# Conditioning pieces 4 and 5 moved ahead in a hybrid diffusion trunk kernel

## The reference, cut to what matters

```
def _adaln(cond, w, b):
    m = jax.nn.silu(cond) @ w + b
    return [t[:, None, :] for t in jnp.split(m, 6, axis=-1)]   # shift, scale, gate for mixer and feed-forward
...
hp = _modulate(_rms(xp, norm_mix[l]), m_ctx[0], m_ctx[1])      # x * (1 + scale) + shift
... mixer: layer 0 attention and short conv, layer 1 Conformer convolution
xp = xp + m_ctx[2] * op
hp = _modulate(_rms(xp, norm_ffn[l]), m_ctx[3], m_ctx[4])
... layer 0: dense SwiGLU (2816 wide); layer 1: top-2 of 8 experts (3584 wide each)
xp = xp + m_ctx[5] * fp

def _conformer_conv(h, p):
    z = h @ p["w_pw1"] + p["b_pw1"];  a, g = jnp.split(z, 2, axis=-1);  u = a * jax.nn.sigmoid(g)
    u = depthwise_conv(u, 31 taps) + p["b_dw"];  u = jax.nn.silu(_layernorm(u, p["ln_g"], p["ln_b"]))
    return u @ p["w_pw2"] + p["b_pw2"]
```

## Time and profile before

| what | value |
| --- | --- |
| three runs | 1481.68, 1483.83, 1489.67 us; median 1483.83 |
| the profiled execution's own time | 1483.04 us |
| its span, first to last instruction | 1481.3 us |
| granted TensorE clock, mean | 0.996 |
| TensorE busy | 1439.8 us (97%) |
| VectorE, ScalarE, GpSimd busy | 1148.8, 935.3, 59.2 us |
| bytes moved | 478.93 MB, mean 323 GB/s |

### The profile page before, as it was taken

The page is one execution under the profiler, slowest core; times in us unless marked ns, Lnnn a source line. Parts: engine busy times, 40 slices in busy tenths (PEclk is TensorE's granted clock), DMA queues, the critical chain, the costliest instruction groups (busy, mean ns, idle before and its releaser), DMA issues.

```text
span 1481.3 us, 20338 instructions
## 1 busy us (share of the span) xinstructions
PE 1439.8 (97%) x8408; PEld 1211.8 (82%) x8408; DVE 1148.8 (78%) x1075; ACT 935.3 (63%) x888; POOL 59.2 (4%) x61
## 2 busy tenths in 40 slices
PE   6999999999989999999999999999999999999997
PEld 4778899998967778888888888888888888888885
DVE  3565744445876699889978989888888987988997
ACT  2454643333415687777777777787777777777773
POOL 0210000001221100000000000000000000001010
PEclk9999999999999999999999999999999999999999
DMA  9867766656795499999989999989999999999993
GB/s 371 300 239 276 266 226 228 228 181 224 245 300 181 156 360 373 373 387 375 378 349 374 373 379 380 377 337 391 376 369 394 373 377 348 376 373 381 400 402 135
DMA packets 103570, 478.93 MB, mean 323 GB/s; under 512 B 8556, under 2 KB 39420, under 8 KB 54320
## 3 DMA queue, kind: packets, MB, share of 16 engines
q1 hardware_dynamic: 99696, 465.86, 82.9%
q0 software_dynamic: 3200, 10.98, 2.3%
q10 hardware_dynamic: 576, 0.73, 0.2%
HBM read 471.91 MB, written 5.63 MB: 322 GB/s over the span
## 4 chain that ended last, share of the span: by engine, by line
PE 87%; DVE 6%; DMA 3%; ACT 2%; issue 1%; POOL 0%; ACTq 0%; DVEq 0%; POOLq 0%
PE bank L1728 19%; PE bank L1726 19%; PE bank L1727 19%; PE bank L1732 5%; PE bank L1734 5%; PE bank L1733 5%; DVE low L1591 2%; PE bank L2276 2%; PE bank L1769 1%; PE bank L2064 1%; PE bank L2065 1%; PE bank L2066 1%; PE bank L2110 1%; PE bank L1786 1%; PE bank L2241 1%
## 5 line engine op out<-in xcount | busy, mean ns | idle before, releaser
L1591 DVE TENSOR_TENSOR low<-raw,high 128x2048 fp32r<-128x2048 f32 x333 | 750.4, 2288 | 106.8 <-ACT high L885 104.9
L885 ACT ACTIVATE high<-raw 128x2048 fp32r<-128x2048 f32 x333 | 632.2, 1921 | 115.5 <-DMA raw<-moe 113.4
L1726 PE MATMUL bank<-high,hidH 128*128 128x512 f32 x896 | 349.5, 390 | 0.0
L1728 PE MATMUL bank<-high,hidL 128*128 128x512 f32 x896 | 349.1, 390 | 0.0
L1727 PE MATMUL bank<-low,hidH 128*128 128x512 f32 x896 | 348.6, 389 | 0.0
L1732 PE MATMUL bank<-hidH,high 128*128 128x256 f32 x736 | 212.3, 289 | 6.0 <-DVE hidL L1050 4.3
L1734 PE MATMUL bank<-hidH,low 128*128 128x256 f32 x736 | 208.8, 284 | 0.0
L1733 PE MATMUL bank<-hidL,high 128*128 128x256 f32 x736 | 208.8, 284 | 0.0
L1728 PEld LDWEIGHTS bank<-high,hidL 128*128 128x128 f32 x896 | 168.2, 188 | 35.0
L1726 PEld LDWEIGHTS bank<-high,hidH 128*128 128x128 f32 x896 | 168.2, 188 | 34.7
L1727 PEld LDWEIGHTS bank<-low,hidH 128*128 128x128 f32 x896 | 168.2, 188 | 34.6
(11 more groups left out here) (249 smaller groups left out, 1216.1 us busy)
## 6 DMA issues: line engine op xcount, KB each, us to landing
raw<-moe SPq DMA_DIRECT2D x336, 1024.0 KB, 5.4
raw<-ada_w SPq DMA_DIRECT2D x40, 1024.0 KB, 5.8
raw<-ffn_gu SPq DMA_DIRECT2D x44, 512.0 KB, 4.9
raw<-ffn_down SPq DMA_DIRECT2D x11, 1024.0 KB, 4.9
raw<-ada_first SPq DMA_DIRECT2D x8, 1024.0 KB, 14.6
raw<-w_in SPq DMA_DIRECT2D x8, 1024.0 KB, 9.0
raw<-conv_pw SPq DMA_DIRECT2D x16, 512.0 KB, 5.2
raw<-w_o SPq DMA_DIRECT2D x4, 1024.0 KB, 6.1
```

The costliest lines, as they stand in the source:

```text
L885: a.activation(high[:, m % SPLITS, :], raw[:, n % RAWS, :], ACT.Copy).then_inc(S("high_ready"), 1)
L1591: v.tensor_tensor(low[:, n % RAWS, :], raw[:, n % RAWS, :], high[:, m % SPLITS, :].bitcast(F32), ALU.subtract).then_inc(S("low_ready"), 1)
L1726: pe.matmul(out, xh, wh, start=start, stop=False)
L1728: return pe.matmul(out, xl, wh, start=False, stop=stop)
```

## The change

Five conditioning pieces of group 3 are used one unit earlier (units 1 to 5 instead of 2 to 6), and their sum one unit earlier. Pieces 0 to 2 of group 4 are used in feed-forward units 8 to 10. The four places around the norm now hold pieces 3 to 6 of group 4. In `pw1`, unit 0 has the last piece of group 4, unit 1 its sum, and units 2 and 3 the first two pieces of group 5; in the convolution one conditioning piece is left, ahead of tile 6. The loads in `plan()` follow that order. VectorE's `rows_out` and `mod_out` of groups 3 and 4 stand earlier as well.

```diff
@@ plan()
-        if 2 <= u <= 6:
-            ada(3, u + 1, u + 2)
+        if u <= 5:
+            ada(3, u + 2, u + 3)
+        if u >= 8:
+            ada(4, u - 8, u - 7)
     order.append(("ffn", "d", FFN_UNITS - 1))
-    ada(4, 0, 3)
+    ada(4, 3, 6)
     order.extend([("pw1", "a", 0), ("pw1", "b", 0)])
-    ada(4, 3, 5)
+    ada(4, 6, 8)
     for u in range(1, 4):
         order.extend([("pw1", "a", u), ("pw1", "b", u)])
-        ada(4, 4 + u, 5 + u)
-    ada(5, 0, 6)
+        if u == 2:
+            ada(5, 0, 1)
+    ada(5, 1, 6)
@@ VectorE, feed-forward units
+                if u == 6:
+                    rows_out(3)
                 if u == 7:
-                    rows_out(3)
-                if u == 8:
                     mod_out(3)
@@ VectorE, pw1 and convolution
-            conv_taps(0, 0, 1, 0, 8)
+            conv_taps(0, 0, 1, 0, 4)
+            rows_out(4)
+            conv_taps(0, 4, 1, 4, 4)
             named("pw1", "b", 2)
             named("pw1", "a", 3)
             glu(1)
+            mod_out(4)
...
             conv_taps(0, 23, 2, 7, 4)
-            rows_out(4)
             conv_taps(0, 27, 2, 11, 4)
-            mod_out(4)
@@ TensorE, feed-forward units
-                    if 2 <= u <= 6:
-                        ada_piece(3, u + 1)
-                    if u == 8:
+                    if u <= 5:
+                        ada_piece(3, u + 2)
+                    if u == 7:
                         ada_sum(3)
+                    if u >= 8:
+                        ada_piece(4, u - 8)
             ffn_down(FFN_UNITS - 1, (1, 3, 5))
-            ada_piece(4, 0)
+            ada_piece(4, 3)
...
-            ada_piece(4, 1)
+            ada_piece(4, 4)
...
-            ada_piece(4, 2)
-            ada_piece(4, 3)
+            ada_piece(4, 5)
+            ada_piece(4, 6)
@@ TensorE, pw1 units
-                ada_piece(4, 4 + u)
+                if u == 0:
+                    ada_piece(4, KT - 1)
+                if u == 1:
+                    ada_sum(4)
+                if u >= 2:
+                    ada_piece(5, u - 2)
@@ TensorE, convolution
             conv_tile(3)
             conv_tile(4)
-            ada_sum(4)
             conv_tile(5)
-            ada_piece(5, 0)
-            ada_piece(5, 1)
+            ada_piece(5, 2)
             conv_tile(6)
             conv_tile(7)
-            ada_piece(5, 2)
```

## The result

The changed kernel took 1493.59 us (median of 9 runs, 1491.62 to 1496.83), the kernel before 1485.25 us on the same occasions. The ratio is 1.0061, with a 95% interval from 1.0049 to 1.0072: slower by 7 to 11 us. The forecast was 1492.8 us. The profiled execution took 1492.57 us against 1483.04, 9.5 us more.

The account below looks back on a forecast made before the run. TensorE, busy 97% of the span, was taken as the bound. Terms +2.36 + 6.17 + 2.1 + 0.6 - 1.0 - 0.5 = +9.7 us on 1483.04 gave 1492.8 us, range 1485.5 to 1496.5.

Parts of the forecast that it names:

- `pw1` a0's load behind the product of unit 10: Feed-forward unit 10: the later load delays silu and down product 10, +6.17 us, of which 0.99 is piece 4.2.
- Pieces 4.0 and 4.1: Feed-forward units 8 and 9: each added piece costs 1.18 us where TensorE has no gap, +2.36 us.
- The clock behind the stall: Down product 10: low clock lasts 4.3 us into it and doubles what runs there, +2.1 us (0 to 2.5).
- Norm and `pw1`: Pieces, sum and VectorE work moved there cost 0, up to +0.5 us if VectorE makes `glu(2)` late.
- b0's late copy: In the norm: b0 arrives some 6 us later, but the late down product holds back the squares as much; 0.
- rival A: Unit 10: the late load costs nothing, kernel not slower beyond +2.7 us, 1485.7 us; chance 0.14.
- Convolution: Low clock +0.6, piece behind tile 7 -1.0, transfers -0.5 us; <kept> gives the forecast as -0.9.
- The piece behind tile 7: Convolution: the conditioning piece there lies on the path and goes away, -1.0 us.
- The transfers: Convolution: `pw2` loads leave earlier, away from the last reads of `shifted`, -0.5 us, within -5 and +2.7.
- the low clock: Convolution, tile 6: idle time grows from 3.3 to about 5 us and low clock covers the first 4.3, +0.6 us.
- Rival B: Convolution: transfers no longer crawl and `shifted` comes in time, total +4.3 us, 1487.3 us; chance 0.12.
- The experts' stage: Experts: TensorE is full, nothing lost or won earlier changes there; a length change above 1 us would be wrong.

Follow-up runs that it names:

- e1: Changed kernel with `pw1` a0 and conditioning piece 4.5 swapped in the list of loads, so a0 loads earlier; ratio 1.0036 to the kernel before.
- e2: Changed kernel with ScalarE's copy and VectorE's subtraction of `pw1` a0 moved behind the activations of unit 10, load still late; ratio 1.0032 to the kernel before.
- e3: Kernel before with conditioning piece 4.3 loaded ahead of `pw1` a0 and b0, no piece used elsewhere; ratio 1.0062.
- e7: Changed kernel with `pw1` a0 and b0 both one place earlier in the list of loads, piece 4.5 behind them; ratio 1.0003 to the kernel before.
- e4: Changed kernel with SP holding loads from the second piece of `pw2` on until the last four reads of `shifted` landed; ratio 1.0037 to the kernel before.
- e8: Changed kernel with `pw1` a0 and b0 loaded one place earlier, and loads from `pw2`'s second piece held until `shifted` landed; 0.9972, 1480.82 us against 1484.64.
- e11: Kernel before with only the hold: loads from the second piece of `pw2` on wait until `shifted` has landed; ratio 0.9998.
- e5: Kernel before with pieces 4.4 and 4.5 moved into the norm's idle time and 5.2 ahead of tile 6; ratio 0.9995.
- e9: Kernel before with 4.4, 4.5 in the norm, 5.2 ahead of tile 6, group 4's sum ahead of tile 3, 5.0, 5.1 ahead of tile 4, loads held; 0.9988.
- e10: The kernel of e9 without the hold of the loads; ratio 1.0039 to the kernel before.

## Why the prediction was right

- **The step that decides, `pw1` a0's load behind the product of unit 10:** right, shown by e1, e2 and e3. It was forecast at +6.17 us and measured 8.21 - 2.60 = 5.61. From the copy to the down product it is the same 6.37 us in both traces; from the release to the copy the load took 5.03 instead of 5.59 us.
- **Pieces 4.0 and 4.1:** forecast +2.36, measured 2.60 - 0.24 = 2.36 in the profile. Whether they reach the kernel's time is another matter: e7 keeps all three pieces and is not shown to be slower than before.
- **The clock behind the stall:** forecast +2.1, measured 10.70 - 8.21 = 2.49. Down product 10 was slow for 5.7 us, not 4.3, but its matmuls took 1.8 times as long (0.213 against 0.119 us from start to start), not double. The two errors work against each other.
- **Norm and `pw1`:** forecast 0, measured -0.3. The remark that b0's late copy is hidden by the late down product was right, and e1 showed what it costs without that cover: 2.5 us. In rival A I left it out. Without the stall the kernel would not have been at the +2.7 us of that rival, but some 2.5 us higher; e1 and e2 were at 5.3 and 4.7 us.
- **Convolution:** forecast -0.9, measured 10.03 - 10.41 = -0.4. The piece behind tile 7 gave its 1.0 us (10.99 - 10.03 = 0.96). The other two terms were of the wrong sign or empty. The transfers, for which I gave -0.5, cost 0.6 (10.99 - 10.41); and the low clock, +0.6, cost nothing more: tiles 6 and 7 took 8.71 us, before 8.80. That these two errors mostly cancel is luck. In the trace two loads still ran beside the writing, which took 7.64 us against 8.23, and with one issue fewer in its midst the reading took not less but more, 10.4 us against 9.2. In its first two microseconds the DMA engines still moved 434 and 374 GB/s, in the kernel before 127 and 222, so the two loads seem to have run on into it; why is open.
- **Rival B** was no description of this kernel, but the mechanism is there: e4 and e8 got 3.6 and 4.6 us from the hold. I named the wrong condition. What must be kept away is what runs beside the writing too, and the change left two loads there. In e11, where the hold leaves these two running, it gave nothing.
- **The experts' stage** changed by -0.5 us, within the 1 us allowed.

The sum of the forecast is 9.7 us, that of the profile 9.5, that of the timed runs 9.1 (7.3 to 10.7). The mechanism and its size were right. That the sum came out within 0.2 us of the profile is luck: the stall, the clock, the norm, the convolution and the experts were each off by 0.3 to 0.6 us, in both directions.

That VectorE's `mod_out(4)` moved ahead of the tiles was priced at nothing. It is worth something: in e3 and e5, without that move, TensorE waits 2.2 us for the taps as soon as tile 4 is late.

## What to carry to other kernels

In a ring of buffers that is filled in a fixed order, every insertion changes whose release each later load waits for: list the pairs of before and after, and look at the program of the engine that first touches each piece, since a piece that is wanted late can stand ahead of work that is wanted now. A filler piece moved earlier is also a load released earlier: ask beside which transfer on the critical path it will run, and hold it there if need be. When one late load is mended, look for the one hidden behind it.

## What the runs showed of the hardware that was not expected

- The granted clock stayed at 0.50 for 5.7 us of work behind an idle time of 4.49 us, but for 3.3 us behind one of 4.92 us ahead of tile 6 in the same execution. Ahead of tile 4 an idle time of 2.75 us cost nothing in the changed kernel (the tile took 3.66 us), and in e7 the same 2.75 us were followed by the low clock. The length of the idle time did not set the loss:

```profile
433.30 5.35 PE L2122 MATMUL bank<-shifted,tapU 128*32 128x256 f32 x64 [2.75 <-DMA shifted<-conv_rows]
```

- Four reads of `shifted`, 316 KB each, took from 8.7 us (e9) to 17.4 us (e10) from issue to use, with SP's loads held and not held.
- A GpSimd addition over 128x16 elements (`pw2_gb`, line 522 before) took 5.87 us in e8 and 5.78 us in e4, and 0.21 to 1.02 us in all other kernels here. VectorE was at its taps beside it in the kernel before as well (0.47 us), so that alone is not the cause, which stays open. The addition is on no path here.
